# Retention on a single core: seven-product input projection in 24 units, with the recurrence cut into 16 items that are dealt out between them

## The reference

```python
def retention(h, positions, w_in, w_out):
    q, k, v, g = jnp.split(h @ w_in, [H * dk, 2 * H * dk, 2 * H * dk + H * dv], axis=-1)   # H=4, dk=256, dv=512
    q = apply_rope(q.reshape(B, S, H, dk), positions)
    k = apply_rope(k.reshape(B, S, H, dk), positions) * (dk ** -0.5)
...
    def step(state, inp):
        scores = jnp.einsum('bhqd,bhkd->bhqk', qi, ki) * intra[None]
        o_inner = jnp.einsum('bhqk,bhkv->bhqv', scores, vi)
        o_cross = jnp.einsum('bhqd,bhdv->bhqv', qi, state) * q_decay[None, :, :, None]
        new_state = state * chunk_decay[None, :, None, None] + jnp.einsum(
            'bhkd,bhkv->bhdv', ki * k_decay[None, :, :, None], vi)
...
    o = (of * lax.rsqrt(jnp.mean(of * of, axis=-1, keepdims=True) + NORM_EPS)).astype(h.dtype)
    o = o.reshape(B, S, H * dv) * jax.nn.silu(g)
    return o @ w_out
```

## Time and profile before

| | |
|---|---|
| median of 3 runs | 2658.11 us (2656.07 to 2658.18) |
| profiled execution, own time | 2658.08 us |
| its span | 2656.2 us |
| PE | 2616.3 us busy, 98% |
| DVE, ACT, POOL | 52%, 33%, 56% |
| DMA | 139.44 MB, mean 52 GB/s |
| mean granted TensorE clock | 0.998 of 2.4 GHz |

### The profile page before, as it was taken

The page is one execution under the profiler, slowest core; times in us unless marked ns, Lnnn a source line. Parts: engine busy times, 40 slices in busy tenths (PEclk is TensorE's granted clock), DMA queues, the critical chain, the costliest instruction groups (busy, mean ns, idle before and its releaser), DMA issues.

```text
span 2656.2 us, 34669 instructions
## 1 busy us (share of the span) xinstructions
PE 2616.3 (98%) x11833; PEld 2159.5 (81%) x11833; DVE 1378.0 (52%) x1740; ACT 869.6 (33%) x1456; POOL 1500.1 (56%) x1334
## 2 busy tenths in 40 slices
PE   8999999999999999999999999999999999999998
PEld 6888888888888788888888788888877888888887
DVE  8333322323325856465563647375678364655644
ACT  4130120121124533333333524234256233333324
POOL 4314323322433478888788644363453788887865
PEclk9999999999999999999999999999999999999999
DMA  4102112111111111211212111111111112112122
GB/s 144 41 28 64 44 32 61 48 36 52 48 44 44 43 54 48 63 47 47 63 53 66 36 49 45 36 56 40 45 56 38 59 48 63 47 47 63 47 68 83
DMA packets 173780, 139.44 MB, mean 52 GB/s; under 512 B 9200, under 2 KB 143472, under 8 KB 173680
## 3 DMA queue, kind: packets, MB, share of 16 engines
q1 hardware_dynamic: 171584, 133.46, 16.8%
q10 hardware_dynamic: 2096, 4.62, 0.5%
HBM read 132.81 MB, written 5.24 MB: 52 GB/s over the span
## 4 chain that ended last, share of the span: by engine, by line
PE 86%; DVE 8%; issue 3%; ACT 2%; DMA 0%; DVEq 0%; SPq 0%; ACTq 0%
PE ps L978 28%; PE ps L982 28%; PE ps L981 28%; DVE residual L2786 2%; DVE f_h_lo L2530 1%; DVE uc L2877 1%; PE ps L1318 0%; DVE h_lo L2326 0%; PE ps L1227 0%; DVE scratch L2307 0%; ACT gate_buf L1628 0%; DVE uc L2871 0%; DVE f_act L2742 0%; DMA residual<-in_x 0%; DVE gate_buf L2882 0%
## 5 line engine op out<-in xcount | busy, mean ns | idle before, releaser
L745 POOL TENSOR_TENSOR f_w_lo<-f_raw,f_w_hi 128x512 fp32r<-128x512 f32 x306 | 434.4, 1423 | 253.1 <-ACT f_w_hi L1837 94.4
L703 POOL TENSOR_TENSOR small<-w_raw 128x1 f32<-128x1 f32 x200 | 54.9, 274 | 792.8 <-PE ps L978 782.3
L978 PE MATMUL ps<-f_h_hi,f_w_hi 128*128 128x512 f32 x1232 | 481.1, 391 | 3.7 <-DVE f_h_lo L2530 2.4
L982 PE MATMUL ps<-f_h_hi,f_w_lo 128*128 128x512 f32 x1232 | 479.6, 389 | 0.0
L981 PE MATMUL ps<-f_h_lo,f_w_hi 128*128 128x512 f32 x1232 | 479.5, 389 | 0.0
L978 PEld LDWEIGHTS ps<-f_h_hi,f_w_hi 128*128 128x128 f32 x1232 | 231.3, 188 | 57.5 <-issue 4.3
L982 PEld LDWEIGHTS ps<-f_h_hi,f_w_lo 128*128 128x128 f32 x1232 | 231.3, 188 | 48.1
L981 PEld LDWEIGHTS ps<-f_h_lo,f_w_hi 128*128 128x128 f32 x1232 | 231.3, 188 | 47.0
L714 POOL TENSOR_TENSOR w_lo<-w_raw,w_hi 128x512 fp32r<-128x512 f32 x190 | 258.7, 1362 | 15.2
L745 POOL TENSOR_TENSOR f_w_lo<-f_sum,f_w_hi 128x512 fp32r<-128x512 f32 x142 | 220.4, 1553 | 60.9 <-ACT f_w_hi L1837 60.9
L978 PE MATMUL ps<-h_hi,w_hi 128*128 128x512 f32 x632 | 249.0, 394 | 0.9 <-DVE h_lo L2277 0.6
(11 more groups left out here) (365 smaller groups left out, 4985.9 us busy)
## 6 DMA issues: line engine op xcount, KB each, us to landing
f_raw<-in_ffn_w_gu SPq DMA_DIRECT2D x176, 256.0 KB, 3.9
w_raw<-in_ret_w_in SPq DMA_DIRECT2D x96, 256.0 KB, 2.8
f_raw<-in_ffn_w_down SPq DMA_DIRECT2D x88, 256.0 KB, 2.9
w_raw<-in_lru_w_in SPq DMA_DIRECT2D x48, 256.0 KB, 2.9
w_raw<-in_ret_w_out SPq DMA_DIRECT2D x32, 256.0 KB, 2.6
w_raw<-in_lru_w_out SPq DMA_DIRECT2D x24, 256.0 KB, 2.8
residual<-in_x SPq DMA_DIRECT2D x8, 512.0 KB, 7.7
out_y<-residual SPq DMA_DIRECT2D x7, 512.0 KB, 2.7
```

The source lines that it names most:

```text
L703: nc.gpsimd.tensor_tensor(small[:, 62:63], col, col, ALU.subtract)
L745: nc.gpsimd.tensor_tensor(lo, src, hi.bitcast(F32), ALU.subtract).then_inc(f_wready, 1)
L978: m = nc.tensor.matmul(o, l_hi, r_hi, start=start, stop=False, skip_group_check=onto)
L982: return nc.tensor.matmul(o, l_lo, r_hi, start=False, stop=stop, skip_group_check=onto)
```

## The change

Retention is rebuilt in the manner of the FFN. `w_in` is cut into 24 units of 256 columns, `IN_ORDER`: for each head two of v (units 4h, 4h+1), one of q and one of k; then eight of g. A unit is seven products (`in_product`) of 4 threes over the seven forms of the normed input, all results transposed (features on partitions). The first norm is `norm_by_halves(RET)`. DVE adds the results up, turns q and k by cos and sin (`turned`, 12 operations), and SP writes each unit to DRAM (`spill`, 4 x 256 KB).

The recurrence is 16 items (head, 256 tokens), in `PARTS`: item m is worked in unit 5 + m, part 0 behind the unit's first product (`keys_and_scores`), part 1 behind the third (`values_turned`), part 2 behind the fifth (`outputs_and_state`), part 3 behind the seventh (`outputs_turned`). q, k and v of an item are loaded back from DRAM (256, 256 and 512 KB) and its output goes there (512 KB). Since v now arrives transposed, it is turned by PE: 8 transposes an item that were not there. The output projection stands behind all units (`out_rows`): 64 weights of 4 threes, for one half of the tokens and then the other; o and g are loaded by heads and halves (8 times 2 MB), and multiplied (`rows_gated`) and split. X is loaded anew, since its place served the tables and these loads. FFNs and RG-LRU are as before.

```diff
+ITEM_PARTS = 4
+FIRST_PART = 35
+PARTS = {}
+for m in range(ITEM_PARTS * ITEMS):
+    PARTS.setdefault(FIRST_PART + m // ITEM_PARTS * PRODUCTS + m % ITEM_PARTS * 2, []).append((m // ITEM_PARTS, m % ITEM_PARTS))
...
+            def keys_and_scores(it):
...
+                pe.wait_ge(r_oc, 2 * it)
...
+                pe.wait_ge(r_qk, 2 * it + 2)
...
+            for r in range(2, IN_UNITS):
+                for p in range(PRODUCTS):
+                    in_product(r, p)
+                    for it, part in PARTS.get(PRODUCTS * r + p, ()):
+                        if part == 0:
+                            keys_and_scores(it)
+                        elif part == 1:
+                            values_turned(it)
+                        elif part == 2:
+                            outputs_and_state(it)
+                        else:
+                            outputs_turned(it)
+            out_rows()
...
+            def item_rounded(it):
+                act.wait_ge(r_qin, 32 * (it + 1))
...
+                nc.scalar.activation(iq_hi[:], q_raw[:], ACT.Copy).then_inc(r_qh, 1)
+                nc.scalar.activation(ik_hi[:], k_raw[:], ACT.Copy).then_inc(r_qh, 1)
...
+            def turn_table(i, out):
+                act.wait_ge(table_arg, i + 1)
...
+            def item_lower(it):
+                dve.wait_ge(r_qh, 2 * it + 1)
+                TT(iq_lo[:], q_raw[:], iq_hi[:].bitcast(F32), ALU.subtract).then_inc(r_qk, 1)
+                dve.wait_ge(r_qh, 2 * it + 2)
+                TT(ik_lo[:], k_raw[:], ik_hi[:].bitcast(F32), ALU.subtract).then_inc(r_qk, 1)
...
+            def projected():
+                angles()
+                turns(4096.0)
+                whole_turns()
+                for i in range(3):
+                    less(i, 4096.0)
+                first_pair_up()
+                turn_arguments()
+                for r in range(2, IN_UNITS):
+                    turn = IN_ORDER[r][0] in "qk"
+                    for p in range(PRODUCTS):
...
+                        if p in (1, 2, 3):
+                            in_sum(r, p - 1)
+                        elif p == 4 and turn:
+                            turned(r, 0, 2)
+                        elif p == 5:
+                            in_less(r, E_C21, j + 1)
+                            if turn:
+                                turned(r, 2, 6)
+                        elif p == 6:
+                            in_less(r, E_C12, j + 1)
...
+                            elif it + 1 < ITEMS:
+                                item_lower(it + 1)
+                        if p == 6 and turn:
+                            turned(r, 6, 12)
...
+            def rows_upper(q):
+                half, h = divmod(q, HEADS)
+                act.wait_ge(r_gated, q + 1)
...
+            def out_ahead(end, done=[3]):
+
+                for w in range(done[0], end):
+                    if w in ROWS_AT:
+                        rows_upper(ROWS_AT[w])
+                    out_round(w)
```

More of the change, by code:

```diff
@@ L321, in query_tile @@
[L321 to L338, removed]
@@ L525, in last @@
                 return u - 1 if restart and j < 2 else u - 2
[L528 to L543, removed]
-                        src = ret_w_out[0][bass.ds(h * DV + k * P, P), nh * 512:(nh + 1) * 512]
-                    load(j % RING, src, None if first and j < RING else
-                         last(h * HEAD_UNITS + j, j, not first))
@@ L578, in pair @@
                     for i, src in enumerate(tile_rows_of(f, 1)):
+                        if first and layer == 0:
+                            sp.wait_ge(f_wready, n.units - 4 + i + 1)
                         if not first and i == 0:
@@ L1502, in ffn, with in_product @@
                     pair(LAST, last=True)
+            def in_product(r, p):
+                j, form, before = PRODUCTS * r + p, H_OF[p], 0 if r == 2 else r - 1
+                if p == 0:
+                    if IN_ORDER[before][0] in "qk":
+                        pe.wait_ge(r_rope, 12 * turned_no(before) + 2)
+                    else:
+                        pe.wait_ge(r_c11, plain_no(before) + 1)
+                elif p < 4:
+                    pe.wait_ge(f_ev, in_ev(before, (None, E_C21, E_C12, E_T6)[p]))
+                elif p == 4:
+                    pe.wait_ge(f_t, r + 1)
+                else:
+                    pe.wait_ge(f_ev, in_ev(r, (E_T5, E_T7)[p - 5]))
+                w_h, w_l = f_unit(j)
+                pe.wait_ge(f_wready, j + 1)
+                for k in range(4):
+                    w, h = slice(k * P, (k + 1) * P), h_cut(form, k)
+                    m = three(in_bank(r, p), w_h[:, w], w_l[:, w], H_hi[:, h], H_lo[:, h],
+                              p < 4 and k == 0, k == 3, onto=p >= 4)
+                m.then_inc(f_mm, 1)
@@ new lines, in values_turned @@
+            def values_turned(it):
+                c = it % N_CHUNKS
+                pe.wait_ge(r_vin, 16 * (it + 1))
+                pe.wait_ge(r_mask, it + 1)
+                if c < N_CHUNKS - 1:
+                    pe.wait_ge(r_kt, chunks_before(it) + 1)
+                for blk in range(CHUNK):
+                    for d in range(4):
+                        m = nc.tensor.transpose(bank(4 + blk, d * P, P),
+                                                v_raw[:, d * ITEM + blk * P:d * ITEM + (blk + 1) * P], ident[:])
+                    m.then_inc(r_vt, 1)
```

1473 lines of the change are left out of this document (835 added, 638 removed).

## The result

The changed kernel takes 2708.47 us (median of 4 runs, 2707.49 to 2710.53) against 2657.38 before: a ratio of 1.0193, 95% interval 1.0178 to 1.0208. It is slower, as forecast, but by 51 us and not by 18, and outside the range of 2649 to 2704.

A forecast was written before the change was run, and what follows sets the result against it. PE, busy 98% of the span, was taken as the bound. Terms -65.3 + 13.3 + 25 + 6 + 33 + 6 = +18 on 2658.1 gave 2676 us, range 2649 to 2704.

The forecast's parts named there:

- Removed, added: PE's matmul work: 96 threes fewer in the input projection, -65.3 us; 128 transposes of v more, +13.3 us.
- The junctions: Between recurrence items, PE waits for the next item's keys behind late DVE lower parts: +33 us, bounds 5 to 45.
- The six long ones: Waits for keys in six q and k units, DVE's `turned` alternating with POOL: 3.8 us each, 23 in all.
- The clock: PE's slower clock after idle stretches: 1.7 us at the start, 1.7 at the output projection, nothing between items.
- rival 3: PE's clock falls at each long wait between items: six would cost 10 us, giving 2687; chance 0.14.
- The start: Up to unit 2, PE loses 40 us against 16 before, clock included: +25 us, bounds 15 to 35.
- the hole of the norm's second half: At the start, PE idle 3.5 us until squares, root and scaling of the second half end at about 36.
- the signs: Expected in PE's starts: a hole of 3 to 5 us near 32, one of 8 to 9 near 68.
- the hole of the angles: At the start, PE's product (0,6) waits behind DVE's eight angle operations until about 76.5: 8 to 9 us.
- Units 2 to 4: DVE's `turn_arguments` and `turned` alternate with POOL, exceeding a unit's PE time: +6 us, range 2 to 12.
- the forecast's signs of being wrong: Keys' waits under 15 us in all, no angles hole, or PE waiting for `r_vin`, `r_kt` or weights' lower parts.
- The output projection: PE waits at the sixth weight and weight 35 for late-loaded rows, clock included: +6 us, range 0 to 12.

The follow-up runs named there:

- run 2: Changed kernel with the next item's ACT roundings and DVE lower parts one product earlier, behind the unit's sixth product: 2668.7 us, ratio 1.0037.
- run 4: Changed kernel with POOL's eleven operations in each of units 2 to 23 cut to 256 of 512 columns, result not the reference's: 2660.0 us, ratio 1.0011.
- run 1: Changed kernel with four DVE operations of `turned` in q and k units moved behind the next item's lower parts: 2684.1 us, ratio 1.0095.
- run 3: Changed kernel with unused matmuls on PE before each of the six long waits for keys: twelve, 2692.0 us, ratio 1.0131; six, 2694.7 us, ratio 1.0151.
- run 6: Changed kernel with loads of head 2's rows issued before output weights 4 to 7 and unit 23's stores: 2710.6 us, ratio 1.0193.

## Why the prediction was wrong

- **Removed, added:** 160 matmuls fewer, as counted, but PE's work at full speed fell by 42.7 us and not by 52. The same 813.5 to 814 us come out of the profiles of runs 2 and 4. An estimate of where 9 us are: in these views a matmul ends 0.39 us behind its start while the next one of a row starts after 0.23, so each of some 30 additional waits hides 0.16 us (5 us, which belong to the waits), and a first matmul behind a row of transposes holds up the next for 0.31 us (216.33 to 216.64), at some 50 places more (4 us). No run tests this.
- **The junctions:** +33 forecast, 33.6 measured. The six long ones were given 3.8 and are 3.79, by the mechanism named. The v units were given 1.1 and have 0.98, the g units 1.3 and have 1.06; item 0's wait of 1.7 was not in the forecast. Runs 1, 2 and 4 show the cause.
- **The clock, the step that failed.** The sum gave the clock 1.7 us at the start and 1.7 at the output projection, from the one idle stretch in the earlier trace rows, nothing at the junctions, and called losses there rival 3 with a chance of 0.14. Measured: 25.9 us, of which 17.6 behind the six long junctions, 1.7 behind item 0's, 3.6 at the start and 3.0 at the output projection. Two errors lie in it. The chance: the earlier trace rows had an idle stretch of the same length (3.64 us) followed by a slow clock, and no reason was given why six waits of 3.8 should go without. The price: behind a wait of 3.79 PE lost 1.7 us once and 2.8 to 3.4 five times, where rival 3 had 1.7 for each; with the clock at the junctions but at that price the sum would have been 2687, still 21 us short. Run 3 measures it: 16.4 us for six waits that last as long as before. The Trainium skill's "TensorE: Matmul & The Clock Gate", "HAM oscillation — how this bites in real kernels", spoke for that rival; the runs agree: a slower clock behind six of six waits of 3.79 us, though behind none of the nine of 0.98 to 1.06 us.
- **The start:** +25 forecast, about +33 measured (unit 2 at 93.7 after 44.8 us of work, 49 lost against 16), inside the bounds of 15 to 35. The places were right. The 8.7 us by which unit 2 is later than forecast are in the main 3.7 at the hole of the norm's second half (7.2 for 3.5, outside the "3 to 5" of the signs), some 3 at the hole of the angles (11.5 for 8 to 9) and some 2 of clock (3.6 for 1.7). The angles were priced at 7.5, or 9 with POOL in the way, and took 11.3: the first three took 1.63 to 1.79 beside POOL and not 0.7, the last three 1.56 on average and not 1.25.
- **Units 2 to 4:** +6 forecast, 1.5 measured (0.85, 0.40 and 0.23). DVE and POOL did alternate, but no more than these lower parts came late. Waits for them were among the forecast's signs of being wrong; they are there, but small.
- **The output projection:** +6 forecast; 5.8 of waits and 3.0 of clock measured. Run 6 shows that the order of the spill was not the whole cause.
- **Sum:** in the forecast's terms, -52 + 33 + 1.5 + 33.6 + 19.3 + 8.8 = +44.2 against 49.5; 5 us are not assigned in these terms. By kind: the forecast had -52 of work, 66.6 of idle time and 3.4 of clock; measured are -42.7, 66.3 and 25.9. That the idle time came out right as a total is in part luck, since it was too low at the start and too high in units 2 to 4; 22.5 of the 31.5 us by which the forecast was short are the clock, 9 the work.

## What to carry

Where PE is the bound, a long wait costs its length and then again what PE does at half speed behind it, in this kernel 3.79 + 2.9 us on average: look at the length of each hole, and not only at their sum. Place what PE needs next (a small rounding, a lower part) ahead of the long row of DVE operations with both inputs in SBUF, and look at what POOL does in that stretch, because each such operation cost POOL's length as well (1.75 us for 0.68). Half a clock is lost only where PE works: a slow stretch in which PE is idle anyway costs nothing. Of a saving of 52 us in matmuls, as forecast, the first version lost all and 51 more in holes and the slow clock behind them; with the holes moved, 12 of it were left.

## What the runs showed of the hardware

- Idle time of PE and its granted clock: of the nine waits of 0.98 to 1.06 us at the keys in the changed kernel none was followed by a lower clock (in run 1 one such was, that at 592.5), the one of 1.70 us at item 0 was; of six of 2.34 us (run 3) two were, of six of 3.79 us all. Matmuls whose results nobody reads kept the clock at 1.00 there (run 3) and paid for themselves.
- DVE's CAST and TENSOR_SCALAR with one input in SBUF were also slower beside POOL: 1.79, 1.63 and 1.63 us at 70.85 to 75.98, while POOL works from 70.81 to 75.44, against 0.68 and 0.69, and 0.69 at 76.01, when POOL is idle. The prediction had counted only operations with two inputs in SBUF, and gave the page's rule on a single input without its condition. In "SBUF — State Buffer", "Who interferes with whom", the Trainium skill exempts the one-input case only outside certain fast modes, and names casts and tensor_scalar among those that can enter them; the three rows agree, though no run here tells the modes apart.
